# Attention and expert kernel on one core: latent value products with a head's high and low values side by side, unread products, other orders in the experts and the layer norm

## What is computed

```
h = x @ w_in                          # split into latent q, kv, a rotary key, and dq, dk, dv
# A: 8 heads of latent attention, value width 64
p = softmax((qn . kn + qr . kr) * scale);   o_mla = p @ v
# B: 4 heads of differential attention, width 128
p = softmax(q1 . k1 + bias) - lam * softmax(q2 . k2 + bias);   o_d = rms_norm(p @ v)
x = layer_norm(ALPHA * x + concat(o_mla, o_d) @ w_o)
# 16 experts (width 512), two for each token, out of its best group of four
y = sum over e of gates[:, e] * ((silu(x @ w_gate[e]) * (x @ w_up[e])) @ w_down[e])
x = layer_norm(ALPHA * x + y)
```

## Time and profile before

| | us |
|---|---|
| time, median of 3 runs | 786.39 (784.81 to 787.71) |
| the profiled execution's own time | 789.17 |
| its span (first to last instruction) | 785.9 |
| PE busy | 737.5 (94%) |
| DVE busy | 582.2 (74%) |
| ACT busy | 483.5 (62%) |
| POOL busy | 265.9 (34%) |

### The profile page before, as it was taken

One profiled execution on the slowest core, in us unless ns is written; L12 is line 12 of the kernel. 1 busy time (PEld: TensorE's weight loads), 2 busy tenths in 40 slices (PEclk: granted clock), 3 DMA queues, 4 the chain that ended last, 5 costly groups with the idle time before them and its releaser, 6 DMA issues.

```text
span 785.9 us, 12710 instructions
## 1 busy us (share of the span) xinstructions
PE 737.5 (94%) x3844; PEld 613.3 (78%) x3844; DVE 582.2 (74%) x975; ACT 483.5 (62%) x874; POOL 265.9 (34%) x291
## 2 busy tenths in 40 slices
PE   4999999999999799999999899999999999999984
PEld 3898888888887577768787677888877777777862
DVE  6965365557555766684878799889988888889657
ACT  3334355557554745675137277788888878888635
POOL 3132356656664333344311114222222222222111
PEclk9999999999999789999998999999999999999998
DMA  9724311222144933321745759999999999999763
GB/s 342 251 108 134 120 58 44 61 68 68 37 133 141 324 155 121 122 75 46 298 173 207 260 195 397 392 370 381 387 372 388 378 374 377 384 388 377 250 214 160
DMA packets 71484, 179.35 MB, mean 228 GB/s; under 512 B 11687, under 2 KB 28071, under 8 KB 71444
## 3 DMA queue, kind: packets, MB, share of 16 engines
q1 hardware_dynamic: 66692, 166.34, 56.0%
q0 software_dynamic: 4752, 12.51, 6.4%
HBM read 153.20 MB, written 30.42 MB: 234 GB/s over the span
## 4 chain that ended last, share of the span: by engine, by line
PE 58%; DMA 19%; DVE 11%; ACT 5%; issue 3%; POOL 2%; SPq 1%; ACTq 0%; DVEq 0%; POOLq 0%
PE bank L649 34%; DMA rawG<-in_w_gate 16%; PE bank L1777 4%; PE bank L1779 3%; PE bank L1778 3%; DVE eGl L1932 2%; PE bank L784 2%; DMA wv_raw<-in_w_in 2%; PE bank L1800 1%; PE bank L1798 1%; PE bank L1799 1%; PE bank L2157 1%; ACT eGh L1862 1%; DMA dv_l<-dv_low 1%; POOL me L1269 1%
## 5 line engine op out<-in xcount | busy, mean ns | idle before, releaser
L1932 DVE TENSOR_TENSOR eDl<-rawD,eDh 128x1024 fp32r<-128x1024 f32 x68 | 80.2, 1219 | 12.3 <-ACT eDh L1862 12.1
L1269 POOL TENSOR_SCALAR me<-me,mrec 128x512 f32<-128x512 f32 (+1 forms) x48 | 65.6, 1368 | 52.2 <-DVE mrec L1448 52.1
L1932 DVE TENSOR_TENSOR eUl<-rawU,eUh 128x1024 fp32r<-128x1024 f32 x68 | 78.8, 1219 | 2.6 <-ACT eUh L1862 2.6
L1932 DVE TENSOR_TENSOR eGl<-rawG,eGh 128x1024 fp32r<-128x1024 f32 x64 | 75.5, 1220 | 5.9 <-ACT eGh L1862 5.0
L2055 POOL DMA_INDIRECT acc_rows<-yg,idx_s x16 | 29.7, 1858 | 135.5 <-ACT yg L1887 135.5
L1862 ACT ACTIVATE eGh<-rawG 128x1024 fp32r<-128x1024 f32 x64 | 65.7, 1058 | 7.4 <-DMA rawG<-in_w_gate 6.9
L1862 ACT ACTIVATE eDh<-rawD 128x1024 fp32r<-128x1024 f32 x64 | 64.0, 1055 | 0.0
L1777 PE MATMUL bank<-eGh,xgT_h 128*128 128x512 f32 x136 | 55.9, 411 | 8.5 <-DVE xgT_l L1937 7.4
L1862 ACT ACTIVATE eUh<-rawU 128x1024 fp32r<-128x1024 f32 x64 | 62.8, 1052 | 0.0
L1777 PE MATMUL bank<-eUh,xgT_h 128*128 128x512 f32 x136 | 54.6, 401 | 0.0
L1779 PE MATMUL bank<-eGl,xgT_h 128*128 128x512 f32 x136 | 53.3, 392 | 0.0
(11 more groups left out here) (346 smaller groups left out, 2185.4 us busy)
## 6 DMA issues: line engine op xcount, KB each, us to landing
rawG<-in_w_gate SPq DMA_DIRECT2D x68, 512.0 KB, 15.5
rawU<-in_w_up SPq DMA_DIRECT2D x68, 512.0 KB, 12.2
rawD<-in_w_down SPq DMA_DIRECT2D x68, 512.0 KB, 13.6
wb_raw<-in_w_in SPq DMA_DIRECT2D x8, 512.0 KB, 4.6
wo_raw<-in_w_o SPq DMA_DIRECT2D x8, 512.0 KB, 7.6
xln_rows<-res SPq DMA_DIRECT2D x6, 512.0 KB, 3.8
dqk_high<-st_h SPq DMA_DIRECT2D x8, 384.0 KB, 2.3
dqk_low<-st_l SPq DMA_DIRECT2D x8, 384.0 KB, 3.3
```

What stands on the lines that cost most here:

```text
L1269: nc.gpsimd.tensor_scalar(e, e, mrec[:, g % NSB:g % NSB + 1], None, ALU.mult).then_inc(m_p, 1)
L1932: nc.vector.tensor_tensor(wl_[X][i][:], raw_of(X, t, i)[:], f32(wh_[X][i][:]), ALU.subtract).then_inc(s_lo[X], 1)
```

## The change

1. *Values side by side.* A new tile `v_hl` holds for each key tile and head the 64 high columns and the 64 low columns of its values next to each other. `product` multiplies them with `pT_h` and with `pT_l`: two products for each key tile, not three. The lower and upper 64 rows of the bank then hold the products of the high and the low values, and their sum is wanted (the product low × low is now contained in it). ACT's `mix_moved` copies the half that is not at the head's rows to `mixM_sum`, DVE's `mix_summed` adds the other one from the bank and frees it; then ACT's `mix_high` and DVE's `mix_low` split the sum, reading SBUF. `mix_high` stands behind the exponentials of the same slot, `mix_low` one slot later. The counts of `m_mh` and `m_ml` double. The mix tiles are one for each pair of heads.
2. *Unread products.* In the slots z = 0, 1, 2 of the differential attention PE first runs 6, 10 and 4 products of 512 columns into bank 3, which nobody reads.
3. *Expert orders.* ACT's `rows(t − 1)` moves behind the first two highs of D and the high part of the turned tokens. DVE takes all low parts of D(0) before those of G(1), and the first iteration has no path of its own; the last low part of an iteration moves behind `x_low(t + 1, 0)`.
4. *Statistics by halves.* In the second norm each half's `bn_stats` follows its addition.

```diff
@@ -147,14 +147,14 @@
     st_l = at("st_l", 121, [P, TOK], FR)
-    v_h = [at(f"v_h{i}", (132, 18)[i], [P, NT, 4 * VDIM], FR) for i in range(2)]
-    v_l = [at(f"v_l{i}", (144, 24)[i], [P, NT, 4 * VDIM], FR) for i in range(2)]
+    v_hl = [at(f"v_hl{i}", (138, 18)[i], [P, NT, 4, 2 * VDIM], FR) for i in range(2)]
     pT_h = [at(f"pT_h{x}", 178 + 16 * x, [P, SEQS[x][2], SEQS[x][1]], FR) for x in range(2)]
...
     me = [at(f"me{i}", 198 + 2 * i, [P, 512]) for i in range(NME)]
-    mixM_h = at("mixM_h", 126, [P, HEADS // 2, TOK], FR)
-    mixM_l = at("mixM_l", 138, [P, HEADS // 2, TOK], FR)
+    mixM_h = [at(f"mixM_h{c}", 126 + 12 * (c // 2) + 3 * (c % 2), [P, TOK], FR) for c in range(HEADS // 2)]
+    mixM_sum = [at(f"mixM_sum{c}", 132 + 12 * (c // 2) + 3 * (c % 2), [P, TOK]) for c in range(HEADS // 2)]
+    mixM_l = [at(f"mixM_l{c}", 132 + 12 * (c // 2) + 3 * (c % 2), [P, TOK], FR) for c in range(HEADS // 2)]
     mixD_h = at("mixD_h", 162, [P, DH, TOK], FR)
@@ -330,7 +330,8 @@
             vs = slice(2 * g[2], 2 * g[2] + 2)
-            return bank[:].rearrange("p (t n) -> p t n", t=2), v_h[g[1]][:, vs, :], v_l[g[1]][:, vs, :]
+            v = v_hl[g[1]][:, vs, :, :]
+            return bank[:].rearrange("p (t h n) -> p t h n", t=2, h=4), v[:, :, :, 0:VDIM], v[:, :, :, VDIM:2 * VDIM]
         t0, n, _ = SEQS[g[2]]
@@ -373,6 +374,7 @@
         O_LATE[z + 1], O_EARLY[z + 2], O_ADDS_LAST[z + 2] = ((k + 1, 0, 6),), ((k + 1, 6, 12),), k + 1
+    UNREAD = {0: 6, 1: 10, 2: 4}
     WO_FIRST = {-1: (0,), 0: (1,), 1: (2, 3)}
@@ -510,7 +512,7 @@
     def mix_parts(n, c):
-        return ((mixM_h, mixM_l), (mixD_h, mixD_l))[n][0][:, c, :], ((mixM_h, mixM_l), (mixD_h, mixD_l))[n][1][:, c, :]
+        return (mixM_h[c][:], mixM_l[c][:]) if n == 0 else (mixD_h[:, c, :], mixD_l[:, c, :])
@@ -793,12 +795,13 @@
-                wait(pe, m_ml, w)
-            vs = slice((h % 4) // 2 * P, (h % 4) // 2 * P + P)
-            pairs = three([(v_h[h // 4][:, t, vs], v_l[h // 4][:, t, vs], pT_h[x][:, j, :], pT_l[x][:, j, :])
-                           for j, t in enumerate(range(SEQS[x][0] // P, SEQS[x][0] // P + nk))])
-
-            last = products(psum[6][:, 0:n], pairs, 3 * js[0], 3 * js[-1] + 3)
+                wait(pe, m_ml, 2 * w - 1)
+            pairs = []
+            for j, t in enumerate(range(SEQS[x][0] // P, SEQS[x][0] // P + nk)):
+                v = v_hl[h // 4][:, t, h % 4, :]
+                pairs += [(v, pT_h[x][:, j, :]), (v, pT_l[x][:, j, :])]
+
+            last = products(psum[6][:, 0:n], pairs, 2 * js[0], 2 * js[-1] + 2)
             if js[-1] == nk - 1:
@@ -863,7 +866,7 @@
             if g < 2:
-                pe.wait_ge(m_ml, 2 * HEADS)
+                pe.wait_ge(m_ml, 4 * HEADS)
                 pe.wait_ge(m_ptl, MT)
@@ -880,7 +883,7 @@
                 if n == 0:
-                    pe.wait_ge(m_ml, 2 * HEADS if t >= NT_P else 2 * HEADS - 1)
+                    pe.wait_ge(m_ml, 4 * HEADS if t >= NT_P else 4 * HEADS - 2)
                     pe.wait_ge(m_ptl, MT)
@@ -899,7 +902,17 @@
+        def unread_products(n):
+
+            for _ in range(n):
+                nc.tensor.matmul(psum[3][:], mix_parts(0, 0)[0][:, 0:P], mix_parts(0, 1)[0][:, 0:512], start=True, stop=True)
+
         def diff_slot(z):
+            if z == 0:
+                pe.wait_ge(m_ptl, MT)
+                pe.wait_ge(m_mh, HEADS)
+            if z in UNREAD:
+                unread_products(UNREAD[z])
             if 0 <= z < DT:
@@ -1074,12 +1087,19 @@
+        def mix_moved(w):
+            h, x = w // 2, w % 2
+            t0, n, _ = SEQS[x]
+            r, other = (slice(VDIM * i, VDIM * i + VDIM) for i in (h % 2, 1 - h % 2))
+            act.wait_ge(m_pv, w + 1)
+            nc.scalar.activation(mixM_sum[h // 2][r, t0:t0 + n], psum[6][other, 0:n], ACT.Copy).then_inc(m_mh, 1)
+
         def mix_high(w):
...
             r = slice(VDIM * (h % 2), VDIM * (h % 2) + VDIM)
-            act.wait_ge(m_pv, w + 1)
-            nc.scalar.activation(mixM_h[r, h // 2, t0:t0 + n], psum[6][r, 0:n], ACT.Copy).then_inc(m_mh, 1)
+            act.wait_ge(m_ml, 2 * w + 1)
+            nc.scalar.activation(mixM_h[h // 2][r, t0:t0 + n], mixM_sum[h // 2][r, t0:t0 + n], ACT.Copy).then_inc(m_mh, 1)
@@ -1097,10 +1117,14 @@
             w = {0: 2 * h - 2, 2: 2 * h - 1}.get(i, -1) if s < MT - 1 else {MT - 1: 2 * HEADS - 2, MT: 2 * HEADS - 1}[s]
+            if s == MT:
+                mix_high(2 * HEADS - 2)
             if w >= 0:
-                mix_high(w)
+                mix_moved(w)
             if s + 3 < MT:
                 exp(s + 3)
+            if 0 <= w < 2 * HEADS - 2:
+                mix_high(w)
             if s >= MT:
@@ -1162,6 +1186,8 @@
                 diff_exp(z + 3, 1)
+            if z == -1:
+                mix_high(2 * HEADS - 1)
             for c in WO_FIRST.get(z, ()):
@@ -1454,13 +1480,21 @@
+        def mix_summed(w):
+            h, x = w // 2, w % 2
+            t0, n, _ = SEQS[x]
+            r = slice(VDIM * (h % 2), VDIM * (h % 2) + VDIM)
+            total = mixM_sum[h // 2][r, t0:t0 + n]
+            dve.wait_ge(m_mh, 2 * w + 1)
+            nc.vector.tensor_tensor(total, total, psum[6][r, 0:n], ALU.add).then_inc(m_ml, 1)
+
         def mix_low(w):
...
             r = slice(VDIM * (h % 2), VDIM * (h % 2) + VDIM)
-            dve.wait_ge(m_mh, w + 1)
-            nc.vector.tensor_tensor(mixM_l[r, h // 2, t0:t0 + n], psum[6][r, 0:n], f32(mixM_h[r, h // 2, t0:t0 + n]),
-                                    ALU.subtract).then_inc(m_ml, 1)
+            dve.wait_ge(m_mh, 2 * w + 2)
+            nc.vector.tensor_tensor(mixM_l[h // 2][r, t0:t0 + n], mixM_sum[h // 2][r, t0:t0 + n],
+                                    f32(mixM_h[h // 2][r, t0:t0 + n]), ALU.subtract).then_inc(m_ml, 1)
@@ -1477,8 +1511,14 @@
             w = {0: 2 * h - 2, 2: 2 * h - 1}.get(i, -1) if s < MT - 1 else {MT - 1: 2 * HEADS - 2, MT: 2 * HEADS - 1}.get(s, -1)
+            if s == MT:
+                mix_low(2 * HEADS - 2)
             if w >= 0:
-                mix_low(w)
+                mix_summed(w)
+            if s < MT and i in (1, 3) and h:
+                mix_low(2 * h - 2 + i // 2)
+            if s == MT + 1:
+                mix_low(2 * HEADS - 1)
             if s >= MT:
@@ -1895,10 +1935,10 @@
                 high("G", t + 1)
-            rows(t - 1)
             high("D", t, (0, 1))
...
                 x_high(t + 1, 0)
+            rows(t - 1)
@@ -1951,19 +1991,16 @@
             hidden(t - 1)
-            if first_iteration(t):
-                low_part("D", 0, (0, 1))
-                h_low(0)
-                low_part("D", 0, (2, 3))
-            else:
+            if not first_iteration(t):
                 low_part("D", t - 1, (2, 3))
-                h_low(t - 1)
+            h_low(t - 1)
             low_part("U", t)
...
                 low_part("G", t + 1)
-            low_part("D", t, (0, 1))
+            low_part("D", t, (0,))
             if not last:
                 x_low(t + 1, 0)
+            low_part("D", t, (1,))
@@ -1972,6 +2009,7 @@
         low_part("U", 0, (1, 2, 3))
+        low_part("D", 0)
         low_part("G", 1)
@@ -2320,10 +2358,9 @@
                     nc.vector.tensor_tensor(res[:, t, ns], res[:, t, ns], psum[W_BANKS[k % 2]][:], ALU.add).then_inc(s_y, 1)
-                dve.wait_ge(s_y, 12 + 2 * t + 1)
-                nc.vector.bn_stats(stats[:, t % 2, 0, :], res[:, t, 0:HW])
-                dve.wait_ge(s_y, 12 + 2 * t + 2)
-                then(nc.vector.bn_stats(stats[:, t % 2, 1, :], res[:, t, HW:D]))
+                    dve.wait_ge(s_y, 12 + 2 * t + hf + 1)
+                    last = nc.vector.bn_stats(stats[:, t % 2, hf, :], res[:, t, ns])
+                then(last)
                 then(nc.vector.bn_aggr(mv[:, t, :], stats[:, t % 2, :, :].rearrange("p a b -> p (a b)")))
```

## The result

The changed kernel takes 783.52 us (median of 10 runs, 780.59 to 787.04), the kernel before beside it 787.65 us (10 runs): ratio 0.9949, interval 0.9927 to 0.9972, so 4.0 us less (2.2 to 5.7). The forecast was 10.7 us less, and 775.7 us. Direction right; size wrong by more than half. Three of the ten runs of after, the profiled one (786.93 us, span 785.1) among them, took 786.9 to 787.0 us and the other seven 780.6 to 783.7, so its span is only 0.8 us shorter than that of before, and what stage lengths say is checked against the timed runs.

A forecast was written before the change was run, and what follows sets the result against it. PE was taken to bound the latent attention, weights' DMA the experts; 6.6 + 2.4 + 1.5 + 0.2 = 10.7 us less gave 775.7 us against the 786.39 us median, range 770.5 to 783.

The forecast's parts named there:

- What bounds the kernel: Whole kernel: PE bounds the latent attention, not the start of the differential attention; weights' DMA sets the experts' pace.
- What is lost again: Latent attention: new waits of the sample product for its bank eat 1.6 us of the 8.2 us saved.
- part 1's 6.6 us: Latent attention: shorter value products save 8.2 us over heads 0 to 6, less 1.6 us of new waits.
- Rival 2: Latent attention: POOL, ACT and DVE set the stage, half the product saving goes (4.1 left), total 778.2 us; chance 0.1.
- What it adds: Latent attention: 16 more ACT (7.7 us) and 16 more DVE instructions (8.8 us), counted at nothing under PE's time.
- Head 7: Last latent attention head, behind 251 us: ACT's new copies against a shorter product, taken as nothing, bounds −1.5 to 1.
- Part 2: Start of differential attention: unread products hold PE's clock, DVE is next bound; gain 2.4 us, bounds 0 to 5.
- signs of being wrong: PE over 5 us idle in latent attention; POOL's ee over 2 us there; new half clock; expert turns over 18.8 us.
- POOL and the shared port: Latent attention: 16 new DVE low parts could each hold up POOL 0.4 to 0.7 us; nothing taken in the sum.
- Part 3: Experts: U load leaves 0.8 us earlier, final xgT_l wait loses 0.7; gain 1.5 us, bounds −1 and 2.5.
- Rival 4: Experts: later row scalings delay scatter and gather, 17 us more if landing takes 10.5, total about 794 us; chance 0.05.
- Part 4: Second norm: first half's statistics fill DVE's idle time between the additions; gain 0.2 us, 0 to 0.6.

The follow-up runs named there:

- e5: Kernel after, with GpSimd's wb_l moved from the fifth to the sixth slot of a head, behind the low queries: 782.71 us, ratio 0.9928.
- e7: Kernel after, with wb_l moved behind the low queries and mix_high moved to the end of its slot: 781.60 us, ratio 0.9925.
- e3: Kernel before with only the new expert orders: 786.47 us, ratio 0.9976.
- e4: Kernel before with only the second norm's statistics by halves: 786.06 us, ratio 0.9981.
- e8: Kernel after without the values side by side (unread products, expert orders and statistics kept): 781.77 us, ratio 0.9926.
- e9: Kernel after, with the third and fourth heads' query and key loads issued earlier and values awaited only by their products: 780.85 us, ratio 0.9919.
- e1: Kernel before with only the values side by side: 789.18 us, ratio 1.0014.
- e10: Kernel after with wb_l behind the low queries (except head h = 3), mix_high at its slot's end and early loads: 776.47 us, ratio 0.9847.
- e11: Kernel after with all mends (wb_l, mix_high, early loads) but three value products as before: 780.28 us, ratio 0.9896.
- e12: Kernel after with all mends, but ACT's row scalings back in front of the D highs: 777.24 us, ratio 0.9862.
- e2: Kernel before with only the 20 unread products: 784.30 us, ratio 0.9943.

## Why the shorter products gave so little in their stage

In the earlier trace rows DVE's second raw queries waited 2.92 us for POOL's low queries. In after the same wait is longer and ends at the same time (timelines of DVE and of POOL, at the end of the second head):

```profile
150.33 0.42 DVE L1461 TENSOR_TENSOR q_raw<-bank,rope_t 128x256 f32<-128x256 f32 x1 [3.38 <-POOL q_l L1276]
...
143.46 1.57 POOL L1295 TENSOR_SCALAR me<-me,mrec 128x512 f32<-128x512 f32 x1 [1.93 <-DVE mrec L1474]
145.02 2.41 POOL L1276 TENSOR_TENSOR wb_l<-wb_raw,wb_h 128x1024 fp32r<-128x1024 f32 x1
147.40 1.57 POOL L1295 TENSOR_SCALAR me<-me,mrec 128x512 f32<-128x512 f32 x1
148.93 1.29 POOL L1276 TENSOR_TENSOR q_l<-q_raw,q_h 128x512 fp32r<-128x512 f32 x1
```

POOL's four instructions run back to back from 143.46 to 150.22, and DVE goes on at 150.33. The first of them waits for exponentials of scores that stand in PE's order ahead of the head's prompt products. So the prompt products, 0.93 of the 1.17 us, lie beside this queue and not in it; only the sample's 0.24 is in the head's cycle. From one such wait of DVE to the next, 129.92 to 150.33, it is 20.41 us, before (129.46 to 150.28) 20.82: 0.41 less, nearer to 0.24 than to 1.17. The second finding is on ACT (timelines of ACT, POOL and PE, at the end of the fourth head):

```profile
191.86 0.63 ACT L1102 ACTIVATE mixM_h<-mixM_sum 64x512 fp32r<-64x512 f32 x1 [1.91 <-DVE mixM_sum L1489]
192.51 0.42 ACT L1059 ACTIVATE q_h<-q_raw 128x256 fp32r<-128x256 f32 x1
...
193.01 0.74 POOL L1276 TENSOR_TENSOR q_l<-q_raw,q_h 128x256 fp32r<-128x256 f32 x1 [1.49 <-ACT q_h L1059]
193.73 1.56 POOL L1295 TENSOR_SCALAR me<-me,mrec 128x512 f32<-128x512 f32 x1
...
195.35 0.66 PE L786 MATMUL bank<-ident,me 128*128 128x128 f32 x4 [0.85 <-POOL me L1295]
```

ACT stands in its new rounding and waits for DVE's sum, which is behind the raw queries, which wait for POOL. Queued behind it are the high queries, POOL's low ones, a normalisation, and PE. In this stage of after ACT waits so in 11 places; before has no such wait (waits of ACT, 112 to 252 us):

```profile
ACT mixM_h L1102 <- DVE mixM_sum L1489: 11.6, 11, 2.1
```

Two edits take one queue each:

```diff
@@ GpSimd, mla_slot (e5) @@
-                if i == 4 and h in NEXT_BLOCK:
-                    block_weights_low(NEXT_BLOCK[h])
                 if i == 5 and h + 2 < HEADS:
                     q_low(h + 2, 0)
+                if i == 5 and h in NEXT_BLOCK:
+                    block_weights_low(NEXT_BLOCK[h])
@@ ScalarE, mla_slot (e6) @@
-            if 0 <= w < 2 * HEADS - 2:
-                mix_high(w)
...
             if s in V_SLOTS:
                 high(("V", 1, V_SLOTS[s]))
+            if 0 <= w < 2 * HEADS - 2:
+                mix_high(w)
```

> The kernel after, with GpSimd's low part of the next block's weights (wb_l, 2.41 us) moved from the fifth to the sixth slot of a head, behind the low queries q_l. Theory A (POOL's queue is on the head's cycle): DVE's second q_raw of heads 1, 2, 5 and 6 comes some 2 us earlier against the slot, PE's waits for q_raw (0.48, 0.61, 0.98, 0.63 us) are gone, and the stage 112 to 252 us is 2 to 3.5 us shorter than in the kernel after (137.6 between the first turn and the last but three). Rival (ACT and DVE handshakes of the new sums are what holds PE): these waits stay or come back at the sample product, stage within 0.7 us of after.

Measured: 782.71 us (ratio 0.9928). The four waits for `q_raw` are gone. The stage is 1.70 us shorter than after's, less than expected, as a new wait came in front of the head without a block of its own, where the weights are wanted at once (waits of PE, 112 to 252):

```profile
PE bank L651 <- POOL wb_l L1276: 3.0, 1, 3.0
PE bank L846 <- issue: 1.3, 1, 1.3
PE bank L651 <- DVE k_l L1451: 1.0, 1, 1.0
PE bank L786 <- POOL me L1295: 0.4, 1, 0.4
```

> The kernel after, with ACT's mix_high moved to the end of its slot, behind the high queries. Theory H (ACT stands 1.8 to 1.9 us in mix_high, waiting for DVE's sum, and with it the high and low queries and the normalisation behind them are late): the waits of PE for me near 188 and 195 us (0.54, 0.85 us) and some of those for k_l go, stage 1 to 2 us shorter than after; the waits for q_raw of the other heads stay. Rival (POOL's wb_l alone): nothing changes by over 0.4 us.

Measured: 783.37 us (ratio 0.9932). The stage is 0.74 us shorter, under the 1 to 2 expected and above the rival's 0.4; the wait for `me` at 195 is gone, that near 188 stays (0.54).

> Both moves of e5 and e6. If both queues held back the gain of the value products, the stage is now 4 to 6 us shorter than before's, PE idles under 1 us in it in all. The total falls by that only if the wait for the last head's values near 330 us doesn't take it back: it hangs on the products themselves, so it should not: 2 to 4 us faster than the kernel after. Rival (PE is again bound by another chain, exponentials and turns): under 2 us of gain in the stage.

Measured: 3.24 us less than before in the stage, where 4 to 6 were expected: the 3.0 for `wb_l` is still there. The total, 781.60 us (ratio 0.9925), is 2 us under after by medians; the ratio intervals of e5, e6 and e7 all overlap with that of after, so for each of the three it is the stage length that speaks. The 69.31 us from the eighth to the last turn of its profile hold the wait of the next section.

## Where the profiled execution lost it again

Chain of waits of after, and PE's timeline at its end:

```profile
322.61 8.23 DMA dv_l<-dv_low
330.84 0.04 issue
330.88 0.50 PE bank L846 x2
```
```profile
330.88 0.50 PE L846 MATMUL bank<-dk_h,dq_h 64*128 64x512 f32 x2 [2.35 <-DMA dv_l<-dv_low]
...
331.94 1.01 PE L859 MATMUL bank<-ident,pp 128*128 128x128 f32 x4
```

The fourth head's operands are six transfers behind one semaphore. SP issues them when the product two heads back is done. PE stands 2.35 us for them, and the clock falls (the mean of 332 to 336 us is 0.58; before it was 1.00 there, with a wait of 0.70). That makes the 3.1 us which this profiled execution lost between the eighth and the last turn.

The wait is not the price of the gain in front, since the start of the load moved with that gain. SP's issues in before and in after (timelines of SP), with what followed in before (chain of waits, timeline of PE):

```profile
322.37 0.33 SPq L549 DMA_DIRECT2D dq_h<-dqk_high  x1
322.74 0.43 SPq L549 DMA_DIRECT2D dq_l<-dqk_low  x1
```
```profile
319.59 0.33 SPq L551 DMA_DIRECT2D dq_h<-dqk_high  x1
319.96 1.18 SPq L551 DMA_DIRECT2D dq_l<-dqk_low  x1
```
```profile
324.64 7.34 DMA dv_l<-dv_low
```
```profile
332.03 0.50 PE L843 MATMUL bank<-dk_h,dq_h 64*128 64x512 f32 x2 [0.70 <-DMA dv_l<-dv_low]
```

The first issue comes 2.78 us earlier in after, but from there to PE's product it is 11.29 us, before 9.66: the second issue takes 0.75 us longer, and the last transfer lands 0.89 us later behind its issue. In all ten kernels with this load in its old place the wait is the time from first issue to product less 8.94 to 8.97 us. It is 1.09 us in e3 and 1.28 in e4, which gain nothing in front, and 0.73 in e8, which gains 4.2 us in front; e7 has 2.00 and after 2.35. So how long the load takes in that execution sets the wait. Why it takes longer in some is open.

The timed runs fit this: they give 4.0 us less, about what was won up to the eighth turn (0.93 + 2.35), and not 0.8. That most executions of after are without the fall of the clock is not shown, since only one was traced. The edit of e9:

```diff
-        sp.wait_ge(s_pv, NT)
-        load_diff(2)
-        sp.wait_ge(s_pv, 2 * NT)
-        load_diff(3)
+        for h in (2, 3):
+            sp.wait_ge(s_bias, 2 * NT * (h - 1))
+            load_dqk(h)
+            sp.wait_ge(s_pv, NT * (h - 1))
+            load_dv(h)
```

Here `load_dqk` and `load_dv` are the two halves of `load_diff`; PE waits for the second at the head's first product.

> The kernel after, with the loads of the third and fourth head's queries and keys of the differential attention issued as soon as the scores two heads back are read (they stood in SP's queue behind a wait for that head's last product), and the values awaited only by their own products. Theory W (this wait takes back what the stages in front gain: 2.35 us at 330.88 and the half clock behind it): no wait for this DMA near 304 or 330 us, clock 1.00 from 320 to 345, the stretch from the eighth to the last turn of this attention 66.4 us or less instead of 69.5, in the total 2 to 3.5 us faster than after. Rival (the stretch is bound elsewhere): under 1 us.

Measured: 780.85 us (ratio 0.9919), 2.7 us under after by medians, though the intervals of the two ratios overlap. PE no longer waits for these operands, the stretch to the last turn is 65.64 us (3.85 shorter than in the profiled execution of after, 0.78 shorter than in before and e8, where the load came soonest), and the clock holds; 320 to 345 us:

```profile
320.00:345.00 25.00, 24.00 (x157) 18.78 (x156) 19.46 (x55) 18.46 (x57) 9.75 (x18) 1.00 0.12 33
```

## The parts in mended company

> Parts 2, 3 and 4 without part 1 (three value products as before). From the single runs (part 1 alone +1.1 us, parts 2, 3, 4 alone -4.5, -1.9, -1.5 us against before): if they add, 780 us, which is 3 to 4 us faster than the kernel after. If part 1 is a gain in company (its products in a stage that ends 0.9 us earlier), this is 0.5 to 1 us slower than after.

Measured: 781.77 us (ratio 0.9926), 1.8 us under after by ratio, not 3 to 4, but on the expected side. The two intervals overlap, so the stage lengths have to decide: without part 1 the attention stage is 0.98 us longer (140.90 against 139.92), and the stretch to the eighth turn 1.83 us shorter (42.01 against 43.84). That makes 0.85 us as the cost of part 1 in the change as it stands, near the 1.0 of e1 (0.95 won, 1.97 lost). The row behind it is DVE's, in the slots where the last units' highs stand in ACT's queue:

```profile
266.38 0.42 DVE L1496 TENSOR_TENSOR mixM_l<-mixM_sum,mixM_h 64x256 fp32r<-64x256 f32 x1 [1.42 <-ACT mixM_h L1102]
266.83 0.69 DVE L1549 CUSTOM_DVE_ANT_0 ee<-bank,bias_t 128x512 f32<-128x512 f32 x1
```

e10 has the edits of e5 (but `wb_l` stays in its slot in the head h = 3, where e5 and e7 had the wait of 3.0 us), e6 and e9.

> The kernel after with all mends: wb_l behind the low queries except in the head in front of the short one (where e5 and e7 gave a new wait of 3.01 us), mix_high at the end of its slot, early loads as in e9. If the queues were what ate the value products' saving, the stage from the first turn to the first scores of the differential attention is 135 to 136 us (before 140.85, after 139.92), and the time 776 to 779 us. Rival (another chain takes over): stage over 137.2.

Measured: 776.47 us (ratio 0.9847), 11.0 us under before beside it, and some 7 to 8 under after (7.1 by medians, 8.0 by ratios). The stage is 135.42 us, 5.43 less than before: with the queues out of the way the shorter products pay. Of the 8.2 us of products, 2.8 still don't show, and PE has these waits left in the stage, 4.4 us:

```profile
PE bank L658 <- DVE k_l L1462: 1.8, 2, 1.1
PE bank L853 <- issue: 1.3, 1, 1.3
PE bank L793 <- POOL me L1304: 0.9, 2, 0.5
PE bank L658 <- DVE pT_l L1491: 0.4, 1, 0.4
```

> As e10, but with three value products as in the kernel before (no part 1). Theory: PE was bound in that stage without them, so moving wb_l gives nothing here: stage 140 to 141 us; boundary 42 us; 779 to 781 us. So part 1 in mended company is worth 2 to 4 us. Rival (moving wb_l is a gain by itself): stage under 139.5.

Measured: 780.28 us (ratio 0.9896), stage 140.91. Moving `wb_l` gives nothing where PE has all its products, so the queue was covered before the change. So the shorter stage of e10 is the work of part 1 and not of the moves. Part 1 is worth 3.8 us here (780.28 − 776.47, the lowest run of e11 above the highest of e10): 5.49 in its stage less 1.79 at the boundary is 3.7.

> As e10, but with ACT's row scalings back in front of the D highs. Theory G (behind them, they put the gather on the loop's path, 18.35 us a turn): turns of 17.8 us come back in the first half and 18.8 in the second, PE waits for xgT_l and not for xg; total within 1 us of e10 since both sums are nearly equal (15 turns: 275.3 against 275.3). Rival (only the order on DVE makes the 18.35): turns stay at 18.3.

Measured: 777.24 us (ratio 0.9862) against 776.47, not to be told apart. Turns of 17.8 us come back (seven of them) and then 18.8, and PE's waits of 470 to 730 us are, in e12 and in e10:

```profile
PE bank L1828 <- DVE xgT_l L1988: 4.4, 7, 0.7
```
```profile
PE bank L1813 <- DMA xg<-x_rows,idx_g: 3.2, 11, 0.4
```

So it is the place of the row scalings that sets which of the two loops one has, and their sums are nearly equal (284.8 and 285.2 us).

## The prediction, step by step

- *What bounds the kernel.* "PE is busy in all of the time, so a product less there is its time less, as long as what feeds PE keeps up": the condition carried it all, and was checked against busy shares (55 to 62%), which say nothing of a queue's order. The stage gave 0.93 us for 6.6, and e10, with the queues moved, 5.43.
- *What is lost again.* The failing step, part 1's 6.6 us. It took the only new wait to be that of the sample product for its bank and priced it at 1.6 us; no such wait is among those listed for PE in the stage of after. And it let DVE's 2.92 us of waiting for POOL stand as a detail. That row was the bound: it says that the queue through POOL ends just when PE needs it. Rival 2 named this chain, but as taking half and at 0.1; together with ACT's wait for DVE's sum it took 7.3 of the 8.2 us.
- *What it adds.* "I count their busy time at nothing" was right for busy time (e10 carries all of it), wrong for the wait: "nothing waits for them" holds for the data, not for what is queued behind the waiting instruction on ACT. The prices in after: `mixM_sum` 0.60 and 0.38 us on ACT, 0.68 and 0.41 on DVE, as taken. Reading SBUF, for which no row had a price, was a little dearer: ACT's `mixM_h` 0.63 and 0.42 in place of 0.59 and 0.37, DVE's wide `mixM_l` 0.79 in the stage in place of 0.68.
- *Head 7.* "I take nothing", bounds −1.5 to 1: it cost 1.8 (e8 against after) to 2.0 us (e1 against before), just outside.
- *Part 2.* Mechanism right, the clock holds; the size by DVE's busy time, 2.4, was too low: 4.2 us by itself (e2), since more than the one stretch moves. In the change it shows as 2.35 only because head 7 takes 1.8 of it. Its hit on 2.4 is chance.
- *Behind it.* The forecast had no step for the loads of the later heads. The wait for them is in the trace of before, 0.70 us, and wasn't looked at. It swings between 0.70 and 2.35 us with the time that the load takes. Two of the prediction's own signs of being wrong came true in the profile of after: over 5 us of PE's idle time in the stage (7.18), and a half clock somewhere new (332 to 336 us).
- *POOL and the shared port.* This hold-up didn't come. In the stage of after each of the 13 new low parts ran while POOL was in a normalisation, which reads SBUF too, and POOL's took the 1.57 and 0.93 us that they take before. DVE's took 0.41 to 0.42 us for the narrow ones and 0.71 to 0.82 for the wide ones, which take 0.69 with POOL idle (one of e10 took 1.14). By the rule that the Trainium skill's "SBUF — State Buffer", "Who interferes with whom", states, one should have waited for the other; these rows don't agree with it, and the measurement decides. At the 2.50 us of the earlier trace rows DVE's operation was of 128x1024 and had begun before POOL's (275.04, POOL 275.22), while in the stage POOL had begun first each time; no run here separates size from order.
- *Part 3.* U's load was to leave 0.8 us earlier than 464.68; it left at 464.63, though the first gathered rows were turned 0.8 us earlier. The D loads did leave earlier (447.3, before 458.7), and nothing waited for them. At the loop's end the 0.74 us for `xgT_l` are gone, with 0.35 for `xg` in their place. The runs of e3 give 1.9 us (0.6 to 3.2), so the 1.5 may be right as a number; the way there was not the one forecast. Rival 4's mechanism came true, PE waits for the gather, at a price of 0.3 us a turn that the turns of 18.8 before make up for.
- *Part 4.* 0.2 us forecast, 0.3 to 0.4 by the traces, 0.3 to 2.6 by the runs: right.

## What to carry over

A stage in which one engine is 100% busy can still have a second chain of nearly the same length; before pricing a saving on that engine, follow the longest wait of the other engines in the stage through one whole period, and count only what lies in that cycle. A wait costs what is queued behind it on its engine, even if nobody wants its result. And one profiled execution can have a slow load, a fall of the clock, or both: before a loss in it is laid to the change, the same stretch should be compared in several kernels and with the timed runs.

## What was not expected of the hardware

A wait of 2.35 us of PE in the middle of a stage at full clock was followed by some 4 us near half clock (mean 0.58), and the stretch around it was 3.1 us longer than before's. A wait of 2.00 us at the same load in e7 also brought a fall (mean 0.93 over 320 to 345 us, as in after); one of 1.39 us in e5 left the clock at 1.00. In after and in e7 the clock was 0.50 for some 3 us from about 1 us behind the wait. And 20 products that nobody reads, 4.6 us of PE work, shortened the time by 4.5 us (e2, interval 2.4 to 6.5).
